# A one-core decoder layer: six stores of new value rows moved behind the weighing of the cached values, and the cached value tiles loaded in a mixed order

## What is computed

```python
def mix_sample(x, win_k, win_v, sb_k_pool, sb_v_pool, mem_k, mem_v, page_table, mw):
    ...
    qa, ka, va, qb, kb, vb, qm = project_heads(rms_norm(x, g_pre), w_in)
    ...
    o_a = combine_by_denominators([dilated_group_gather(qa, k_all, v_all, n_buf, w, d) for w, d in DIL_PATTERNS])
    k_past = sb_k_pool[page_table].reshape(B, n_past, N_HEADS_SB, HEAD_DIM)
    v_past = sb_v_pool[page_table].reshape(B, n_past, N_HEADS_SB, HEAD_DIM)
    ...
    o_b = sweep_query_blocks(lambda q, qp: stick_breaking_block(q, kb_all, vb_all, qp, sb_bias), qb, pos)
    o_m = memory_attention(qm, mem_k, mem_v)
```

## Time and profile before

| | |
|---|---|
| median of 3 runs | 2264.4 us (2260.56 to 2265.96) |
| the profiled execution | 2271.01 us, of which the trace spans 2269.2 us |
| PE busy, of the span | 2153.5 us (95%) |
| PE weight loads | 2042.6 us (90%) |
| DVE busy | 1340.9 us (59%) |
| ACT busy | 919.0 us (40%) |
| POOL busy | 429.5 us (19%) |
| bytes read and written in HBM | 447.95 MB and 8.62 MB, 201 GB/s over the span |

### The profile page before, as it was taken

The page is one execution under the profiler, slowest core; times in us unless marked ns, Lnnn a source line. Parts: engine busy times, 40 slices in busy tenths (PEclk is TensorE's granted clock), DMA queues, the critical chain, the costliest instruction groups (busy, mean ns, idle before and its releaser), DMA issues.

```text
span 2269.2 us, 41305 instructions
## 1 busy us (share of the span) xinstructions
PE 2153.5 (95%) x16769; PEld 2042.6 (90%) x16769; DVE 1340.9 (59%) x3210; ACT 919.0 (40%) x1171; POOL 429.5 (19%) x369
## 2 busy tenths in 40 slices
PE   7999999999999999999967879899999999999996
PEld 6999999999999999999842339799999999999996
DVE  6555545555555686777783426575545565555656
ACT  3544434444343455343312414454434344343443
POOL 5200000000000043677501100440000000000004
PEclk9999999999999999999989979899999999999999
DMA  7454555555555546999999975345555555555551
GB/s 262 168 186 171 182 176 178 186 173 180 186 177 177 185 167 244 332 339 349 317 273 314 278 205 176 130 171 183 186 174 180 186 178 176 185 182 174 184 184 41
DMA packets 221536, 459.24 MB, mean 202 GB/s; under 512 B 11466, under 2 KB 12363, under 8 KB 220571
## 3 DMA queue, kind: packets, MB, share of 16 engines
q1 hardware_dynamic: 219874, 452.32, 59.2%
q0 software_dynamic: 1472, 4.29, 0.5%
HBM read 447.95 MB, written 8.62 MB: 201 GB/s over the span
## 4 chain that ended last, share of the span: by engine, by line
PE 49%; DMA 4%; DVE 3%; SPq 2%; issue 1%; POOL 1%; ACT 0%; POOLq 0%; DVEq 0%; ACTq 0%
PE ps L503 15%; PE ps L505 15%; PE ps L504 15%; DMA v_cache<-win_v 1%; SPq L427 1%; PE ps L809 1%; DMA v_cache<-sb_v 1%; SPq L426 1%; PE ps L684 1%; POOL acc L1736 1%; DVE y L1288 1%; DVE k_cache L1453 1%; DMA v_cache<-mem_v 1%; DMA k_cache<-win_k 0%; PE ps L782 0%
## 5 line engine op out<-in xcount | busy, mean ns | idle before, releaser
L1242 DVE TENSOR_TENSOR wl<-raw,wh 128x1024 fp32r<-128x1024 f32 x592 | 732.9, 1243 | 703.7 <-ACT wh L889 702.8
L889 ACT ACTIVATE wh<-raw 128x1024 fp32r<-128x1024 f32 x656 | 691.6, 1059 | 1029.6 <-PE ps L505 1005.1
L503 PE MATMUL ps<-xh,wh 128*128 128x264 f32 (+1 forms) x3776 | 1081.3, 286 | 17.7 <-DVE xl L1254 9.4
L505 PE MATMUL ps<-xh,wl 128*128 128x264 f32 (+1 forms) x3776 | 1077.9, 285 | 0.0
L504 PE MATMUL ps<-xl,wh 128*128 128x264 f32 (+1 forms) x3776 | 1077.8, 285 | 0.0
L503 PEld LDWEIGHTS ps<-xh,wh 128*128 128x128 f32 x3776 | 715.2, 189 | 20.8 <-issue 9.0
L505 PEld LDWEIGHTS ps<-xh,wl 128*128 128x128 f32 x3776 | 715.4, 189 | 0.0
L504 PEld LDWEIGHTS ps<-xl,wh 128*128 128x128 f32 x3776 | 714.9, 189 | 0.2
L503 PE MATMUL ps<-hh,wh 128*128 128x264 f32 x1408 | 400.8, 285 | 0.0
L505 PE MATMUL ps<-hh,wl 128*128 128x264 f32 x1408 | 399.9, 284 | 0.0
L504 PE MATMUL ps<-hl,wh 128*128 128x264 f32 x1408 | 399.1, 283 | 0.0
(11 more groups left out here) (227 smaller groups left out, 1159.8 us busy)
## 6 DMA issues: line engine op xcount, KB each, us to landing
raw<-w_gu SPq DMA_DIRECT2D x176, 1024.0 KB, 4.9
raw<-w_down SPq DMA_DIRECT2D x88, 1024.0 KB, 5.0
raw<-w_in SPq DMA_DIRECT2D x40, 1024.0 KB, 7.5
v_cache<-sb_v SPq DMA_DIRECT2D x128, 256.0 KB
k_cache<-sb_k SPq DMA_DIRECT2D x84, 256.0 KB
raw<-w_out SPq DMA_DIRECT2D x16, 1024.0 KB, 5.4
head_space<-sb_k SPq DMA_DIRECT2D x44, 256.0 KB
raw<-w_mem_kv SPq DMA_DIRECT2D x8, 1024.0 KB, 5.4
```

The lines of the kernel that those rows point to most:

```text
L503: pe.matmul(out, w_hi, rh(k0 + kk), start=first and kk == 0, stop=False)
L505: mm = pe.matmul(out, w_lo, rh(k0 + kk), start=False, stop=last and kk == 1)
L889: act.activation(wh[:, c % UNIT_SLOTS], raw_unit(c), ACT.Copy).then_inc(hi_made, 1)
L1242: dve.tensor_tensor(wl[:, c % UNIT_SLOTS], raw_unit(c), wh[:, c % UNIT_SLOTS].bitcast(F32), ALU.subtract).then_inc(lo_made, 1)
```

## The change

Three things are changed together. The value tiles of all kinds are loaded and weighed in a mixed order: the 8 page tiles of sequence 0, then in turns two page tiles of the next sequence and one window or memory tile of this one, and at the end the four window and memory tiles of sequence 7. There are 10 value slots instead of 7; the three new ones (`late_values`) lie where key slots lay, so SP waits for the last key (`k_used`) before it uses them. The sums go round three PSUM banks (5, 6, 7) instead of two. And POOL stores the six blocks of new prompt values behind the heads' sums of squares and a wait for the last weighed value tile, no longer as ACT copies them.

```diff
-V_SLOTS = 7
+V_SLOTS = 10
...
 def value_tile(t):
 
-    if t < SB_TILES:
-        return divmod(t, PAGES // 2)
-    b, k = divmod(t - SB_TILES, 4)
-    return b, PAGES // 2 + k
+    if t < PAGES // 2:
+        return 0, t
+    b, r = divmod(t - PAGES // 2, 12)
+    if b == DEC - 1:
+        return b, PAGES // 2 + r
+    return (b + 1, r // 3 * 2 + r % 3) if r % 3 < 2 else (b, PAGES // 2 + r // 3)
...
+SUM_ORDER = [(0, 0)] + [(kind, b + 1 - kind) for b in range(DEC - 1) for kind in range(2)] + [(1, DEC - 1)]
...
     b, k = value_tile(t)
-    return b if k < PAGES // 2 else DEC + b
+    return SUM_ORDER.index((int(k >= PAGES // 2), b))
...
             sums = sb("sums", [P, 2, 512], F32, part)
+            late_values = sb("late_values", [P, 3, 1024], F32, part)
...
             for t in range(TILES):
+                if t == V_SLOTS - 3:
+                    sp.wait_ge(k_used, TILES)
                 if t >= V_SLOTS:
                     sp.wait_ge(v_weighed, t - V_SLOTS + 1)
-                load_tile(*value_tile(t), v_cache[:, t % V_SLOTS], v_loaded[t % V_SLOTS], sb_v, win_v, mem_v)
+                load_tile(*value_tile(t), value_slot(t), v_loaded[t % V_SLOTS], sb_v, win_v, mem_v)
...
-                if k in (0, PAGES // 2) and number >= 2:
-                    pe.wait_ge(sum_taken, number - 1)
+                if k in (0, PAGES // 2) and number >= 3:
+                    pe.wait_ge(sum_taken, number - 2)
...
-                    mm = pe.matmul(ps[5 + number % 2][32 * q:32 * q + 32, :], by, values, start=first, stop=last)
+                    mm = pe.matmul(ps[5 + number % 3][32 * q:32 * q + 32, :], by, values, start=first, stop=last)
...
+            late_stores = []
...
-                else:
-                    store(dst, v_rows[:, t, 512 * (grp - 3):512 * (grp - 3) + 512])
+                elif t < 2:
+                    late_stores.append((dst, t, grp))
...
+            pool.wait_ge(v_weighed, TILES)
+            for dst, t, grp in late_stores:
+                store(dst, v_rows[:, t, 512 * (grp - 3):512 * (grp - 3) + 512])
```

More of the change, by code:

```diff
@@ L157, in decoder_step @@
         with ExitStack() as part:
-            v_cache = sb("v_cache", [P, V_SLOTS, 1024], F32, part)
+            v_cache = sb("v_cache", [P, V_SLOTS - 3, 1024], F32, part)
             rows = sb("rows", [P, 2, 512], F32, part)
@@ L291, in key_slot, with value_slot @@
             return head_space[:, 1024 * s:1024 * s + 1024] if s < 2 else k_cache[:, s - 2]
+        def value_slot(t):
+            s = t % V_SLOTS
+            return v_cache[:, s] if s < V_SLOTS - 3 else late_values[:, s - V_SLOTS + 3]
         def row_slot(n):
@@ L793, in weigh_values @@
                 pe.wait_ge(v_loaded[t % V_SLOTS], 32 * (t // V_SLOTS + 1))
-                if k in (0, PAGES // 2) and number >= 2:
-                    pe.wait_ge(sum_taken, number - 1)
+                if k in (0, PAGES // 2) and number >= 3:
+                    pe.wait_ge(sum_taken, number - 2)
                 for j in range(2):
-                    values = v_cache[0:n, t % V_SLOTS, 512 * j:512 * j + 512]
+                    values = value_slot(t)[0:n, 512 * j:512 * j + 512]
                     if k < PAGES // 2:
@@ L1605, in take_sums @@
                     dve.wait_ge(sum_taken, number)
-                    kind, b = divmod(number, DEC)
-                    total, part = sums[:, kind], ps[5 + number % 2][:]
+                    kind, b = SUM_ORDER[number]
+                    total, part = sums[:, kind], ps[5 + number % 3][:]
                     if b == 0:
```

## The result

The changed kernel takes 2250.93 us (median of 5 runs, 2249.09 to 2253.49), the kernel before on the same chip 2265.96 us (median of 5, 2260.56 to 2271.0). The ratio is 0.9938, with a 95% interval from 0.9921 to 0.9955: faster by 15.0 us, where 16.0 us and a time of 2248.4 us were forecast. In the comparisons of the experiments the kernel before has medians from 2261.78 to 2263.76 us over 9 to 23 runs; against these the gain is 11 to 13 us. The two profiled executions are 2271.0 us (the longest run of the kernel before) and 2249.09 us (the shortest of the changed one), so the traces lie 22 us apart, 7 more than the medians. What follows therefore compares stages, and stretches from one event to another.

What follows compares the result with a forecast made beforehand. SP's issue pace bound the value pages, transfers the window and memory tiles. Mixed order 15.4 plus stores 0.6 made 16.0 us less: 2255.0 against the profiled 2271.0, scaled to the median 2248.4 us; range 2236 to 2262.

Steps and rivals of the forecast that it cites:

- Mixed order: Value loads: pages at 363 GB/s, other tiles at 244, together 152.6 us against 168, so 15.4 us less.
- SP is no longer the pace: Mixed value loads: four pages and a window DMA cost SP under 4 us; transfers need longer at every earlier rate.
- Ten slots: Value slots: three more tiles, 4.3 us at 363 GB/s, contained in the 168 us and not added; key wait costs nothing.
- they carry the queue over the hole: Ten value slots keep loads going from 1183 to 1190, where the transfer nearly stopped at 138 GB/s.
- the 168 us: Value stage of the kernel before: time of the value transfers, from 1169 to 1337 us.
- Three banks: PE's value sums: waits for DVE to take the sum three numbers before, costed at nothing.
- Stores gone from the key phase: Around 1120 us: six DMAs, 1.57 MB, leave the key phase, counted as 0.6 us less.
- stores behind the values: POOL's six stores, 3.3 us to issue, behind the last weighed tile: cost nothing, or 4.3 us if `w_out` waited.
- PE's share: Value stage: PE's busy share was to go up from 0.80 to near 0.9.
- Windows run faster too: Rival, value loads: mixed with pages, window tiles also reach 363 GB/s; 2229 us, or 2239 for half; chance 0.15.
- Nothing much happens: Rival, value pages: SP's pace was not the limit, pages stay at 313 GB/s; 2263 us, chance 0.08.
- Slower: Rival, value queue: strided tiles hold up pages, everything at 244 GB/s; 29.7 us more, 2294 us, chance 0.07.

Runs made afterwards that it cites:

- e5: Kernel before, with value pages loaded from fixed places 0 to 127, so SP does no register load between their DMAs: 2250.46 us, ratio 0.9937.
- e9: Kernel before, with the 96-row window value tiles loaded with 128 rows, 2.1 MB more: 2248.46 us, ratio 0.993.
- e2: Kernel before plus only the mixed order and its three banks; 7 slots, stores where they were: 2252.54 us, ratio 0.9954.
- e6: Changed kernel, with value pages loaded from fixed places without register loads: 2245.67 us, ratio 0.9922 to the kernel before.
- e10: Changed kernel, with the 96-row window value tiles loaded with 128 rows: 2229.74 us, ratio 0.9846 to the kernel before.
- e1: Kernel before, with only the six stores moved behind the values: 2264.22 us, ratio 1.0007.
- e4: Changed kernel, with the six stores back at their old place, as ACT copies the rows: 2251.66 us, ratio 0.9952 to the kernel before.
- e7: Kernel before, with the strided window value tiles read from 96 neighbouring rows: 2263.47 us, ratio 1.0002.
- e8: Changed kernel, with the strided window value tiles read from 96 neighbouring rows: 2250.96 us, ratio 0.9948 to the kernel before.
- e3: Kernel before, with only ten value slots; old order, two banks, early stores: 2258.76 us, ratio 0.999.
- e12: e10 with the strided key tiles loaded with 128 rows as well: 2229.49 us, ratio 0.9849 to the kernel before.

## Why the prediction was right

**Mixed order, 15.4 us.** Right in mechanism and place, and in size within a few us. Two limits took turns, SP's pace at the pages and the transfers at the windows, and mixing lets one work while the other would hold. e5 shows the first limit by taking it away, e9 the second, e2 that the order alone is enough. The stretch is 152 us at 313 GB/s, forecast 152.6. That the sum came out within 1 us is partly luck, since two errors in it cancel. I put the pages at 363 GB/s. Alone, with a full queue, they reach 384 (e5), and the mixture would then take 147.6 us at 327 GB/s, the rate that e6 has; in the changed kernel the register loads take 3 to 5 us of that back. "SP is no longer the pace" was thus only nearly true: its bare 4.0 us for a group stand against 4.51 us that the group took. I had priced it under 4 us, and written that the transfers need longer at every rate of the earlier trace rows; at 386 GB/s for both kinds the 1.51 MB of a group take 3.9 us, which is less, and in e10, where both kinds are that fast, SP is indeed at its bare pace. The medians of the longer comparisons put the gain at 11 to 13 us, so the size is right within a few us and not to the decimal.

**Ten slots.** The step "they carry the queue over the hole" came true in the profile (138 to 292 GB/s) and was worth nothing on top of the order: e2, with seven slots and the hole, ends the stage in 161.4 us, as the changed kernel does in 161.5. The term was contained in the 168 us and so in the 15.4; taken apart, the order with its three banks gives all of it that can be told. Where the 1.2 MB that were loaded early went is open: the rate behind the hole is lower with ten slots (314 against 319 GB/s) at a higher busy share (1.04 against 1.01), but no run here shows why.

**Three banks.** Costed at nothing; the waits that the profile shows for PE and its weight loads at value tiles are for DMAs, or "issue", which names nothing waited for. The longest group of each:

```profile
PE ps L822 <- DMA v_cache<-sb_v: 11.8, 16, 3.5
PEld ps L822 <- DMA v_cache<-sb_v: 27.3, 22, 2.5
```

No wait for DVE's sums is among them. No run has the mixed order without the third bank.

**Stores gone from the key phase, 0.6 us, and stores behind the values, 0.** e1 says 2.1 us more with an interval that holds zero, and e4's ratio lies 0.0014 over that of the whole change with the intervals overlapping: neither term can be told from nothing. For the late stores the trace shows no cost: they landed in some 7 us and `w_out` came no later, as the forecast said. That the early ones had cost 0.6 us is not shown.

**PE's share.** 127.03 / 152 = 0.84, forecast near 0.9. A small miss, with the busy time taken over from before: the 586 matmuls that took 135.56 us in the earlier trace rows take 130.94 us now, and PE still waits for values.

```profile
1165.00:1321.00 156.00, 130.94 (x586) 47.83 (x586) 66.99 (x227) 47.06 (x92) 21.39 (x29) 0.95 1.01 306
```

**The rivals.** *Windows run faster too* did not happen by mixing, and its cause is refuted here: with rows next to one another instead of 16 or 64 KB apart the time did not move (1.0002, e7). The Trainium skill (DMA: Bandwidth & Descriptors, Latency and other measured facts) infers that streams at row pitches of large powers of two meet in the same HBM channels; the pitches that it gives as slow, for copies, are of 2 MiB and more. Carried over to the 16 and 64 KB of this case, as the prediction did, the inference would have made e7 and e8 faster, and the measurement speaks against that; for the page's own pitches no run here shows anything. With 128 partitions the kernel reaches 2229.74 us, where the rival had 2229; that the two agree is chance, since the rival had another cause, other bytes and another rate. *Nothing much happens* needed pages at 313 GB/s in any company; e5 shows 384. *Slower* needed the pages to take on the rate of the tile ahead of them, 244 GB/s; the mean of 313 GB/s excludes it.

What stays open, besides the slots: why a transfer of 1024 floats into 96 partitions makes its packets slow. Other partition counts and other row lengths were not tried. Nor is it known why the same window tiles ran at 244 GB/s in some executions and at 266 in e3's.

## What to carry to other kernels

When a stage has two kinds of work in one queue, read for each kind which resource idles: if they idle in turns, mixing the kinds hides one limit behind the other, and the new time is the sum of what the binding resource needs for each. A busy share of 1.0 is no proof that the bytes move as fast as they can: compare the GB/s of stages with the same share, and ask what their tiles have in common. Before reading a gain out of two traces, look where their runs stand among all runs of the kernel: here the trace of the kernel before is its longest run, and its stage says 17.5 us where the medians say 11 to 15. A partly filled tile may be cheaper to load whole, as in e10 and e12, which beat both kernels of this study.

## What the runs showed of the hardware

A stage of value tiles of which half were 96x1024 float32 came in far slower than the same stage with 128x1024 tiles throughout: 0.195 against 0.123 us for a mean packet, 244 against 391 GB/s at the same busy share, and hardly faster (259 GB/s) when the rows were neighbours. If the 128-partition tiles took 391 GB/s in both, the 96-partition ones came at about 162 GB/s, 2.4 us for 384 KB against 1.3 us for 512 KB (an estimate from 14.68 MB in 60.2 us, of which 6.29 MB went to 96 partitions). Loading 2.1 MB that nobody uses made the kernel 15.3 us faster in the old order (e9) and, by the difference of the two gains, 19 us in the new one (e10). SP issued 14 page DMAs into empty slots in 11.37 us with the register loads and in 7.55 us without them (e6), 0.81 against 0.54 us each. Since 0.81 us for 256 KB are 324 GB/s, below the 384 that the engines reached without the loads, taking them away was worth 12.9 us in the old order (e5).
